# Mixer weights of a Conformer and attention trunk: loaded plainly by SyncE and rounded by ScalarE, where GpSimd's queue rounded them in the transfer

## The chip, the cores and the metric

One core of a Trainium2 chip runs the whole program. The metric is device time in microseconds, the median of several executions. "The profile" is one execution taken by the hardware profiler, with its trace.

## What is computed

Two layers; tokens are 512 plus 16 learned meta tokens, the width D is 1024, D_FF is 2816.

```python
for i in range(DEPTH):
    h_res = h_res + 0.5 * swiglu(rms_norm(h_res, ffn1_norm[i]), ffn1_w_in[i], ffn1_w_out[i])
    h = rms_norm(h_res, mix_norm[i])
    proj = h @ w_in[i]
    y_a = conv_module(proj[..., :o_conv], conv_w[i], conv_b[i], conv_ln_g[i],
                      conv_ln_b[i], conv_w_out[i])
    q = rms_norm(proj[..., o_conv:o_q].reshape(B, L, N_Q_HEADS, HEAD_DIM), q_norm[i])
    k = rms_norm(proj[..., o_q:o_k].reshape(B, L, N_KV_HEADS, HEAD_DIM), k_norm[i])
    v = proj[..., o_k:o_v].reshape(B, L, N_KV_HEADS, HEAD_DIM)
    y_b = window_sink_attention(q, k, v, attn_sinks[i]) @ attn_w_out[i]
    gates = jax.nn.sigmoid(proj[..., o_v:] + gate_bias[i])
    merged = gates[..., :D_MODEL] * y_a + gates[..., D_MODEL:] * y_b
    h_res = h_res + merged @ w_out[i]
    h_res = h_res + 0.5 * swiglu(rms_norm(h_res, ffn2_norm[i]), ffn2_w_in[i], ffn2_w_out[i])
return h_res[:, N_META:]
```

The convolution module is a gated unit, a causal depthwise convolution over 31 tokens, a LayerNorm, a swish and a product. Attention sees a window of two chunks of 64 tokens, the meta tokens and a sink for each head. The part between the two SwiGLUs is called a mixer here.

## The kernel before

**Products.** Every large product is made of three: each operand is split into a part `h` rounded to the matmul's type (fp32r) and the rest `l`, and TensorE adds `wh·xh + wh·xl + wl·xh` in PSUM. So weights have two copies in SBUF, `wha`/`whb` (rounded) and `wla`/`wlb` (rest); `wfa`/`wfb` is the same memory as `wha`/`whb`, seen as plain float32.

**A mixer's blocks.** A mixer is 68 blocks of weights, each 1024x128 (512 KB, in SBUF 128 partitions of 1024 values). Blocks 0 to 43 are the input projection, in four groups of 11; in each group TensorE places the attention of four heads between the blocks. Blocks 44 to 51 are the attention's output, 52 to 59 the convolution's output, 60 to 67 `w_out`. TensorE takes a block in `products` (L1074), 48 matmuls of 264 columns, or 24 of 512 where the second layer drops the meta tokens. PSUM holds the results of two blocks in turn, so block n can start only when VectorE has taken the result of block n - 2: in attention's output at L1848, in `w_out` at L1676.

**Weights.** A block has one of four places in SBUF (`mix_units`). Place n % 4 is free when TensorE is through with block n - 4 (`mix_freed`). Then:

- `mix_hi` (L615), on GpSimd's queue: a transfer that casts float32 to fp32r on its way into `wha`;
- `neg` (L666), on ScalarE: `wla` becomes minus `wha`;
- `mix_lo` (L619), on GpSimd's queue: a transfer of the same block that adds into `wla`, which leaves the rest.

GpSimd issues `mix_hi` of block n ahead of `mix_lo` of block n - 1. A wait for a free place thus also holds back the `mix_lo` behind it.

**ScalarE's order** is written out by hand. `neg` of block n stands among the steps of earlier blocks: in a group through the little function `h(i)`, which is `neg` of the block three after block i, and after the groups through `block_hi(n)`, which is `neg(l, n + 1)`. Between them stand the exponentials (L883), the copies of the turned probabilities (`take_windows` L893, `take_metas` L900 and L902), and in the LayerNorm the squares (L1015), the square root (L1020), the swish (L1025) and the rounding of its result (L1028). After L902 TensorE multiplies the probabilities with the values (`mix_values`, L1310 and L1313), three times in a group: after its ninth block, in the middle of its eleventh, and after the first block of the next group. VectorE's loop in the LayerNorm scales by the reciprocal (L1889), takes the rest of each swish result (L1892), and behind the eighth takes two blocks of attention's output (`take_att`, L1848).

**The SwiGLUs' weights** go another way: SyncE's queue loads `raw` pairs of tiles (L543 768 KB, L546 256 KB) and output weights (L552) as plain float32. ScalarE rounds them (L675, L697, L704) and ScalarE or VectorE makes the rest (L679, L1475). Near the end of a mixer ScalarE and VectorE also prepare the first pairs of the second SwiGLU. In a mixer SyncE otherwise copies the keys to the upper partitions (`kw`, L578), once a group, as soon as VectorE has them.

Of the kernel before, what the change touches and what calls it, by code (L numbers as in the profile page):

```python
# [25 lines left out]
ACT = mybir.ActivationFunctionType  # L26
# [3 lines left out]
P = 128  # L30
DEPTH, D, SEQ, META = 2, 1024, 512, 16
CHUNK, HD, CONV_K = 64, 64, 31
# [4 lines left out]
KD, KF = D // P, FF // P  # L37

CHUNKS = ((0, 11), (11, KF))
# [7 lines left out]
GROUPS = NKV  # L47
# [27 lines left out]
GB_N = 11  # L75
# [9 lines left out]
B_CONV, B_MO = B_ATT + KD, B_ATT + 2 * KD  # L85
NBLK = B_MO + KD
# [66 lines left out]
def run_of(j):  # L153

    s = j // KF
    while not begins(s):
        s -= 1
    e = s + 1
    while e < STAGES and not begins(e):
        e += 1  # L160
    return s * KF, e * KF
# [39 lines left out]
USED = {key: n + 3 for n, key in enumerate(tensor_order())}  # L201
# [28 lines left out]
def mix_freed(l, n):  # L230
    if n > 3:
        return USED["mix", l, n - 4]
    if n == 0:
        return USED["P4", (2 * l + 1) * KF - 1]
    if REGION[(2 * l + 1) * KF - 1] == 0:
        return USED[("P7", "P2", "P6")[n - 1], (2 * l + 1) * KF - 1]
    return USED["out", 2 * l, len(CHUNKS) - 1, NB - 4 + n]
# [16 lines left out]
def build(nc, x, params, qk_gain, sinks, pairs, outs6, outs5, mixes, out):  # L254
# [7 lines left out]
    with ctx:  # L262
        def sb(name, shape, dt=F32, at=ctx):
            return at.enter_context(nc.sbuf_tensor(name, shape, dt))

        def sem(name):
            return ctx.enter_context(nc.semaphore(name))
# [44 lines left out]
        mix = ExitStack()  # L312
# [5 lines left out]
        kw = sb("kw", [P, META + NCH * WK], at=mix)  # L318
# [65 lines left out]
        def units(bufs, u, n):  # L384

            t, u = (bufs[0], u) if u < BASE_UNITS else (bufs[1], u - BASE_UNITS)
            return t[:, u:u + n, :, :].rearrange("p u k c -> p (u k) c")

        hi_units, lo_units, f32_units = (wha, whb), (wla, wlb), (wfa, wfb)
# [45 lines left out]
        def mix_units(bufs, n):  # L435
            return units(bufs, MIX_UNITS[n % 4], 2)
# [13 lines left out]
            return ap.rearrange("p k (h n) -> p (k h) n", h=2)  # L450


        w_hi, w_neg = [sem(f"w_hi{s}") for s in range(4)], sem("w_neg")
        w_lo = [sem(f"w_lo{s}") for s in range(4)]
        raw_in, raw22_in = [sem(f"raw_in{s}") for s in range(2)], [sem(f"raw22_in{s}") for s in range(2)]
        prm_in, first_lo, sq_used = sem("prm_in"), sem("first_lo"), sem("sq_used")
# [10 lines left out]
        blk_used = sem("blk_used")  # L467
# [14 lines left out]
        qrms_ready, krms_ready, kn_ready = sem("qrms_ready"), sem("krms_ready"), sem("kn_ready")  # L482
        kn_dup = sem("kn_dup")
# [45 lines left out]
        @block.sync  # L529
        def _(sp):  # L530

            def load_x(k):
                sp.dma_start(resid[:, k, :], x[:, k, :]).then_inc(x_in[k], 16)

            def load_pair(j):

                j0, j1 = run_of(j)
                if j - 2 >= j0:
                    sp.wait_ge(a_hi, j - 1)
                    sp.wait_ge(s_sum, 4 * (j - 1))  # L540
                if j in (2, 3):
                    sp.wait_ge(first_lo, j)
                sp.dma_start(raw[:, j % 2, KP:4 * KP, :], pairs[j, :, KP:4 * KP, :]).then_inc(raw_in[j % 2], 16)  # L543
                if j - 2 >= j0:
                    sp.wait_ge(a22_hi, j - 1)
                sp.dma_start(raw[:, j % 2, 0:KP, :], pairs[j, :, 0:KP, :]).then_inc(raw22_in[j % 2], 16)  # L546

            def load_out(s, c, m):
                count, u, k = out_block(s, c, m)
                sp.wait_ge(blk_used, out_freed(s, c, m))  # L550
                src = (outs6, outs5)[m % 2][(count - 1) // 2, :, :, :]
                sp.dma_start(units(f32_units, u, 2)[:, 0:k, :], src).then_inc(ob_in[m % 3], 16)  # L552

            def stage(s):
                for c, (ta, tb) in enumerate(CHUNKS):
                    for t in range(ta, tb):
                        j = s * KF + t
                        if j + 2 < run_of(j)[1]:
                            load_pair(j + 2)
                        if t == tb - 2:  # L560
                            load_out(s, c, 0)
                        if t == tb - 1:
                            load_out(s, c, 1)
                            load_out(s, c, 2)
                    for b in range(NB - 3):
                        load_out(s, c, b + 3)

            load_x(0)
            load_x(1)
            load_pair(0)  # L570
            for k in range(2, KD):
                load_x(k)
            load_pair(1)
            for l in range(DEPTH):
                stage(2 * l)
                for g in range(GROUPS):
                    sp.wait_ge(kn_ready, l * GROUPS + g + 1)
                    sp.dma_start(kw[HD:P, :], kw[0:HD, :]).then_inc(kn_dup, 16)  # L578

                sp.wait_ge(blk_used, USED["mix", l, B_CONV])  # L580
                load_pair((2 * l + 1) * KF)
                load_pair((2 * l + 1) * KF + 1)
                stage(2 * l + 1)

            for m in range(KD):
                sp.wait_ge(res_done, (STAGES * len(CHUNKS) - 1) * KD + m + 1)
                sp.dma_start(out[:, m, :], resid[:, m, META:]).then_inc(fin_out, 16)
            sp.wait_ge(fin_out, 16 * KD)


        @block.gpsimd
        def _(pool):
            nc.gpsimd.memset(eps64[:, :], HD * EPS).then_inc(const_done, 1)
            nc.gpsimd.memset(ident[:, :], 0.0).then_inc(const_done, 1)
            nc.gpsimd.memset(ones[:, :], 1.0).then_inc(const_done, 1)
            nc.gpsimd.memset(eps1[:, :], EPS).then_inc(const_done, 1)
            pool.wait_ge(const_done, 4)
            nc.gpsimd.affine_select(out=ident[:, :], in_=ident[:, :], compare_op=ALU.not_equal, fill=1.0,
                                    base=0, pattern=[[-1, P]], channel_multiplier=1).then_inc(const_done, 1)

            def base_lo(j):
                pool.wait_ge(a_neg, j - 1)
                pool.dma_start(units(lo_units, U_A[REGION[j]], 2), pairs[j, :, KP:3 * KP, :], accum_op=ALU.add)\
                    .then_inc(a_lo[j % 2], 16)

            def base22_lo(j):
                pool.wait_ge(a22_neg, j)
                pool.dma_start(units(lo_units, U_A22[REGION[j]], 1), pairs[j, :, 0:KP, :], accum_op=ALU.add)\  # L610
                    .then_inc(a22_lo[j % 2], 16)

            def mix_hi(l, n):
                pool.wait_ge(blk_used, mix_freed(l, n))
                pool.dma_start(mix_units(hi_units, n), mixes[l * NBLK + n, :, :, :]).then_inc(w_hi[n % 4], 16)  # L615

            def mix_lo(l, n):
                pool.wait_ge(w_neg, l * NBLK + n + 1)
                pool.dma_start(mix_units(lo_units, n), mixes[l * NBLK + n, :, :, :], accum_op=ALU.add)\  # L619
                    .then_inc(w_lo[n % 4], 16)  # L620

            def stage(s):
                for c, (ta, tb) in enumerate(CHUNKS):
                    j0, j1 = s * KF + ta, s * KF + tb
                    more = j1 < run_of(j0)[1]
                    for j in range(j0, j1):
                        if j + 2 < j1:
                            base_lo(j + 2)
                        if j + 1 < j1:
                            base22_lo(j + 1)  # L630
                    if more:
                        base_lo(j1)
                        base22_lo(j1)
                        base_lo(j1 + 1)

            for l in range(DEPTH):
                stage(2 * l)
                mix_hi(l, 0)
                mix_lo(l, 0)
                mix_hi(l, 1)  # L640
                for n in range(2, NBLK):
                    mix_hi(l, n)
                    mix_lo(l, n - 1)
                    if n == B_MO + 5:
                        base_lo((2 * l + 1) * KF)
                mix_lo(l, NBLK - 1)
                base22_lo((2 * l + 1) * KF)
                base_lo((2 * l + 1) * KF + 1)
                stage(2 * l + 1)
# [3 lines left out]
        def _(act):  # L653
            func = nc.scalar.activation
# [5 lines left out]
            def neg(l, n):  # L660

                if n >= NBLK:
                    return
                s, turn = mix_turn(l, n)
                act.wait_ge(w_hi[s], turn * 16)
                func(mix_units(lo_units, n), mix_units(hi_units, n).bitcast(F32), ACT.Copy, scale=-1.0)\  # L666
                    .then_inc(w_neg, 1)

# [277 lines left out]
            for l in range(DEPTH):  # L946
# [52 lines left out]
                g = GROUPS - 1  # L999
# [963 lines left out]
```

## Time and profile before

| | |
|---|---|
| median of 3 runs | 2389.26 us (2387.78 to 2391.06) |
| the profiled execution | 2391.75 us |
| its span, first to last instruction | 2390.0 us |
| mean granted TensorE clock | 0.990 of 2.4 GHz |
| busy: TensorE, VectorE, ScalarE, GpSimd | 2347.2, 1680.6, 1223.8, 345.4 us |
| moved by GpSimd's queue, by SyncE's queue | 210.53 MB, 145.08 MB |

The mixers run from about 384 to 856 us and from 1579 to 2037 us, the four SwiGLUs before, between and after them. Busy times count instructions, not waits. In the rows of the profile a line number is that of the kernel before; in a timeline the value in brackets is how long the engine stood idle just ahead of the row, and what ended that.

### The profile page before, as it was taken

The numbers are of one execution on the slowest core, as the hardware profiler recorded it, in microseconds if no ns is written. First come the engines' busy times: TensorE is split into PE (matmuls) and PEld (weight loads), VectorE is DVE, ScalarE is ACT, GpSimd is POOL, SyncE is SP. The second block draws the span as 40 slices with busy tenths as digits, with TensorE's granted clock in tenths as the row PEclk, the third lists the DMA queues.
The fourth block names the chain that finished last, engine by engine and source line by source line (L and its number), as shares of the span: only waits on it lengthen the run. The fifth ranks groups of instructions, "written<-read, shape, count | busy, mean of one in ns | idle before, by whom it ended". The sixth has DMA issues, their size and how long they took to land.

```text
span 2390.0 us, 43268 instructions
## 1 busy us (share of the span) xinstructions
PE 2347.2 (98%) x17809; PEld 2232.3 (93%) x17809; DVE 1680.6 (70%) x2732; ACT 1223.8 (51%) x1987; POOL 345.4 (14%) x454
## 2 busy tenths in 40 slices
PE   7999999999999999999999999999999999999999
PEld 6999999999999999999999999999888777898997
DVE  8855854898886478568678558548988855874773
ACT  7734733443445377356467347343434354762751
POOL 1101101111212211011011011011211222110110
PEclk9999999999999999999999999999999999999999
DMA  6845736666667968458458457366776698683753
GB/s 171 183 122 145 168 88 152 147 147 146 149 141 186 214 129 184 112 144 185 110 122 183 126 143 170 88 151 147 151 158 143 139 219 195 141 197 104 164 130 113
DMA packets 111364, 358.70 MB, mean 150 GB/s; under 512 B 12608, under 2 KB 12608, under 8 KB 111168
## 3 DMA queue, kind: packets, MB, share of 16 engines
q0 software_dynamic: 64080, 210.53, 43.2%
q1 hardware_dynamic: 46720, 145.08, 21.1%
q8 instruction: 141, 2.31, 0.4%
q14 instruction: 55, 0.45, 0.1%
q10 hardware_dynamic: 368, 0.33, 0.0%
HBM read 351.41 MB, written 2.10 MB: 148 GB/s over the span
## 4 chain that ended last, share of the span: by engine, by line
PE 85%; DVE 6%; ACT 4%; DMA 3%; issue 2%; DVEq 0%; ACTq 0%; SPq 0%
PE po L1074 27%; PE po L1091 22%; PE po L1142 20%; PE ptr L1091 7%; PE pov L1091 4%; DMA wha<-in_mixes 1%; DVE cv L1691 1%; DMA wla<-in_mixes 1%; PE pov L1310 1%; PE pov L1313 1%; PE pstat L1270 1%; PE pov L1240 1%; DMA wfa<-in_outs 1%; DVE rms L1540 1%; PE ptr L1279 1%
## 5 line engine op out<-in xcount | busy, mean ns | idle before, releaser
L1074 PE MATMUL po<-xh,wha 128*128 128x264 f32 (+1 forms) x1408 | 351.3, 316 | 2.4 <-DMA wla<-in_mixes 1.7
L1074 PE MATMUL po<-xl,wha 128*128 128x264 f32 (+1 forms) x1408 | 341.4, 309 | 0.0
L1074 PE MATMUL po<-xh,wla 128*128 128x264 f32 (+1 forms) x1408 | 339.7, 308 | 0.0
L1691 DVE SCALAR_TENSOR_TENSOR cv<-ub,lp,cv 128x528 f32<-128x528 f32 (+1 forms) x480 | 333.4, 754 | 1.7
L1142 PE MATMUL po<-hh,wha 128*128 128x264 f32 (+1 forms) x1232 | 282.8, 299 | 1.9 <-DVE wla L1483 1.9
L1142 PE MATMUL po<-hl,wha 128*128 128x264 f32 (+1 forms) x1232 | 283.7, 300 | 0.0
L1142 PE MATMUL po<-hh,wla 128*128 128x264 f32 (+1 forms) x1232 | 283.7, 300 | 0.0
L666 ACT ACTIVATE wla<-wha 128x1024 fp32r<-128x1024 f32 x136 | 143.7, 1058 | 232.2 <-DMA wha<-in_mixes 232.1
L1483 DVE TENSOR_TENSOR wla<-wfa,wha 128x768 fp32r<-128x768 f32 (+1 forms) x128 | 113.6, 890 | 202.9 <-ACT wha L704 202.8
L1074 PEld LDWEIGHTS po<-xh,wha 128*128 128x128 f32 x1408 | 232.1, 193 | 23.1 <-issue 6.1
L1074 PEld LDWEIGHTS po<-xh,wla 128*128 128x128 f32 x1408 | 231.3, 192 | 11.5
L1074 PEld LDWEIGHTS po<-xl,wha 128*128 128x128 f32 x1408 | 231.8, 192 | 10.3
L704 ACT ACTIVATE wha<-wfa 128x768 fp32r<-128x768 f32 (+1 forms) x128 | 101.0, 789 | 267.7 <-DMA wfa<-in_outs 267.7
L1091 PE MATMUL po<-x7h,whb 128*128 128x264 f32 (+1 forms) x768 | 221.0, 288 | 17.1 <-ACT tmp L710 6.9
L1091 PE MATMUL po<-x7h,wha 128*128 128x264 f32 (+1 forms) x832 | 236.4, 284 | 0.5 <-DVE tmp L1571 0.5
L1091 PE MATMUL po<-x7l,wha 128*128 128x264 f32 (+1 forms) x832 | 236.4, 284 | 0.0
L1091 PE MATMUL po<-x7h,wla 128*128 128x264 f32 (+1 forms) x832 | 236.0, 284 | 0.0
L1091 PE MATMUL po<-x7l,whb 128*128 128x264 f32 (+1 forms) x768 | 218.1, 284 | 0.0
L1091 PE MATMUL po<-x7h,wlb 128*128 128x264 f32 (+1 forms) x768 | 217.8, 284 | 0.0
L1142 PEld LDWEIGHTS po<-hh,wha 128*128 128x128 f32 x1232 | 196.1, 188 | 10.5 <-DVE wla L1483 2.6
L1142 PEld LDWEIGHTS po<-hh,wla 128*128 128x128 f32 x1232 | 196.9, 189 | 7.5
L1142 PEld LDWEIGHTS po<-hl,wha 128*128 128x128 f32 x1232 | 196.4, 188 | 7.6
(239 smaller groups left out, 5665.6 us busy)
## 6 DMA issues: line engine op xcount, KB each, us to landing
wha<-in_mixes POOLq DMA_DIRECT2D x136, 512.0 KB, 4.4
wla<-in_mixes POOLq DMA_DIRECT2D x136, 512.0 KB, 6.5
raw<-in_pairs SPq DMA_DIRECT2D x88, 768.0 KB, 5.3
wfa<-in_outs SPq DMA_DIRECT2D x64, 384.0 KB, 3.1
wlb<-in_pairs POOLq DMA_DIRECT2D x47, 512.0 KB, 8.6
raw<-in_pairs SPq DMA_DIRECT2D x88, 256.0 KB, 7.0
wla<-in_pairs POOLq DMA_DIRECT2D x87, 256.0 KB, 6.7
wfa<-in_outs SPq DMA_DIRECT2D x64, 320.0 KB, 2.9
```

The costliest lines, as they stand in the source:

```text
L666: func(mix_units(lo_units, n), mix_units(hi_units, n).bitcast(F32), ACT.Copy, scale=-1.0)\
L704: func(units(hi_units, u, 2)[:, 0:k, :], units(f32_units, u, 2)[:, 0:k, :], ACT.Copy).then_inc(ob_hi, 1)
L1074: ins = mm(po[:, 2 * out_slot + h, 0:width], w[:, k, :], v[:, k, t:t + width], start=begin and k == 0 and p == 0, stop=last and k == kt - ...
L1091: ins = mm(bank, a[:, kp, :], b[:, kp, cols7], start=begin and kp == 0 and p == 0, stop=kp == KP - 1 and p == 2, skip_group_check=True)
L1142: ins = mm(po[:, 2 * ps(m) + h, 0:width], w[:, k, :], v[:, t, x:x + width], start=t == 0 and p == 0, stop=t == CHUNK_T - 1 and p == 2, ski ...
L1240: mm(qss[:, pos, :], qsq[:, tok0(pos):tok0(pos) + CHUNK, :].rearrange("p n j -> p (n j)"), halves[:, :], start=True, stop=True)
L1270: ins = mm(score(i, h), q[r, :], kw[r, c:c + WK], start=True, stop=True)
L1279: ins = tr(ptr[:, (2 * n + h) * P:(2 * n + h + 1) * P], pw[:, (b + 1) % 2, at:at + WIN], ident[:, :])
L1310: mm(dst[h * HD:(h + 1) * HD], vw[:, pos - 1, :], cut(pt[:, i, h, :]), start=True, stop=False, skip_group_check=True)
L1313: ins = mm(dst[h * HD:(h + 1) * HD], vz[0:n, i - i0, h, :], cut(ptm[0:n, :]), start=pos == 0, stop=True, skip_group_check=True)
L1483: tt(units(lo_units, u, 2)[:, 0:k, :], units(f32_units, u, 2)[:, 0:k, :], units(hi_units, u, 2)[:, 0:k, :].bitcast(F32), ALU.subtract).the ...
L1691: stt(cv[:, j, a:], u, w, cv[:, j, a:], ALU.mult, ALU.add).then_inc(conv_step, 1)
```

## The change

SyncE's queue loads each mixer block as plain float32 into its place (`load_mix`, into `wfa`, the memory of `wha`), still after `mix_freed`. ScalarE rounds it in place to fp32r, and then negates it into `wla` as before. GpSimd's queue keeps the accumulating transfer alone, in the order of the blocks. On SyncE's queue the load of block 0 goes between the output weights of the first SwiGLU; the others follow its last, and the key copies and the first two pairs of the second SwiGLU get places between the loads.

```diff
@@ @block.sync
+            def load_mix(l, n):
+
+                sp.wait_ge(blk_used, mix_freed(l, n))
+                sp.dma_start(mix_units(f32_units, n), mixes[l * NBLK + n, :, :, :]).then_inc(w_in[n % 4], 16)
+
@@
                     for b in range(NB - 3):
                         load_out(s, c, b + 3)
+                        if b == 0 and s % 2 == 0 and c == len(CHUNKS) - 1:
+                            load_mix(s // 2, 0)
@@
             for l in range(DEPTH):
                 stage(2 * l)
-                for g in range(GROUPS):
-                    sp.wait_ge(kn_ready, l * GROUPS + g + 1)
-                    sp.dma_start(kw[HD:P, :], kw[0:HD, :]).then_inc(kn_dup, 16)
-
-                sp.wait_ge(blk_used, USED["mix", l, B_CONV])
-                load_pair((2 * l + 1) * KF)
-                load_pair((2 * l + 1) * KF + 1)
+                for n in range(NBLK):
+                    if n:
+                        load_mix(l, n)
+                    g, i = divmod(n, GB_N)
+                    if g < GROUPS and i == 8:
+                        sp.wait_ge(kn_ready, l * GROUPS + g + 1)
+                        sp.dma_start(kw[HD:P, :], kw[0:HD, :]).then_inc(kn_dup, 16)
+
+                    if n in (B_CONV + 4, B_CONV + 6):
+                        load_pair((2 * l + 1) * KF + (n - B_CONV - 4) // 2)
                 stage(2 * l + 1)
@@ @block.gpsimd
-            def mix_hi(l, n):
-                pool.wait_ge(blk_used, mix_freed(l, n))
-                pool.dma_start(mix_units(hi_units, n), mixes[l * NBLK + n, :, :, :]).then_inc(w_hi[n % 4], 16)
@@
-                mix_hi(l, 0)
-                mix_lo(l, 0)
-                mix_hi(l, 1)
-                for n in range(2, NBLK):
-                    mix_hi(l, n)
-                    mix_lo(l, n - 1)
-                    if n == B_MO + 5:
+                for n in range(NBLK):
+                    mix_lo(l, n)
+                    if n == B_MO + 4:
                         base_lo((2 * l + 1) * KF)
-                mix_lo(l, NBLK - 1)
@@ @block.scalar, in neg(l, n)
-                act.wait_ge(w_hi[s], turn * 16)
+                act.wait_ge(w_in[s], turn * 16)
+                func(mix_units(hi_units, n), mix_units(f32_units, n), ACT.Copy).then_inc(w_hi, 1)
+                act.wait_ge(w_hi, l * NBLK + n + 1)
                 func(mix_units(lo_units, n), mix_units(hi_units, n).bitcast(F32), ACT.Copy, scale=-1.0)\
                     .then_inc(w_neg, 1)
```

ScalarE's order from the first mixer's LayerNorm on, before: the end of the squares (L1015), the square root into `t`, and the first steps of swish (`cv`) and rounding (`xh`).

```order
L1015 ACTIVATE pw<-cv 128x528 x3
L666 ACTIVATE wla<-wha 128x1024
L1020 ACT_TABLE_LOAD
L1020 ACTIVATE t<-pstat,eps 128x528
L666 ACTIVATE wla<-wha 128x1024
L1025 ACT_TABLE_LOAD
...
L1028 ACTIVATE xh<-cv 128x528
L666 ACTIVATE wla<-wha 128x1024
L1025 ACTIVATE cv<-cv,lp 128x528
```

And of the change, the same place (its lines are three higher, L666 is L669):

```order
L1018 ACTIVATE pw<-cv 128x528 x3
L667 ACTIVATE wha<-wfa 128x1024
L669 ACTIVATE wla<-wha 128x1024
L1023 ACT_TABLE_LOAD
L1023 ACTIVATE t<-pstat,eps 128x528
L667 ACTIVATE wha<-wfa 128x1024
L669 ACTIVATE wla<-wha 128x1024
L1028 ACT_TABLE_LOAD
...
L1031 ACTIVATE xh<-cv 128x528
L667 ACTIVATE wha<-wfa 128x1024
L669 ACTIVATE wla<-wha 128x1024
L1028 ACTIVATE cv<-cv,lp 128x528
```

Each negation has a copy just ahead of it, and nothing else has moved on ScalarE.

SyncE's queue through the first mixer, before: the last output weights of the first SwiGLU, the keys, and the pairs (L543 and L546) of the second SwiGLU.

```order
L552 DMA wfa<-in_outs 128x640
L578 DMA kw<-kw 64x1168 x4
L543 DMA raw<-in_pairs 128x1536
L546 DMA raw<-in_pairs 128x512
L543 DMA raw<-in_pairs 128x1536
L546 DMA raw<-in_pairs 128x512
L543 DMA raw<-in_pairs 128x1536
```

And of the change:

```order
L552 DMA wfa<-in_outs 128x640
L557 DMA wfa<-in_mixes 128x1024 x8
L589 DMA kw<-kw 64x1168
...
L589 DMA kw<-kw 64x1168
L557 DMA wfa<-in_mixes 128x1024 x15
L543 DMA raw<-in_pairs 128x1536
L546 DMA raw<-in_pairs 128x512
L557 DMA wfa<-in_mixes 128x1024 x2
L543 DMA raw<-in_pairs 128x1536
L546 DMA raw<-in_pairs 128x512
L557 DMA wfa<-in_mixes 128x1024 x9
L543 DMA raw<-in_pairs 128x1536
```

A key copy now stands behind the load of its group's ninth block, the first two pairs are two blocks apart, and the third pair stands behind the mixer's last load.

## Rows read from the trace of the kernel before

**Rows 1.** The page: busy time of each engine, its share of the span, instructions

```profile
PE 2347.2 (98%) x17809; PEld 2232.3 (93%) x17809; DVE 1680.6 (70%) x2732; ACT 1223.8 (51%) x1987; POOL 345.4 (14%) x454
```

**Rows 2.** TensorE's waits: engine, output, line <- releaser: us in total, times, longest

```profile
PE po L1074 <- DVE resid L1676: 2.0, 2, 1.4
...
PE po L1074 <- DMA wla<-in_mixes: 1.7, 4, 0.6
...
PE po L1074 <- DVE gb L1848: 0.6, 1, 0.6
```

**Rows 3.** The page's groups: count, busy us, mean ns, idle before and its releaser

```profile
L666 ACT ACTIVATE wla<-wha 128x1024 fp32r<-128x1024 f32 x136 | 143.7, 1058 | 232.2 <-DMA wha<-in_mixes 232.1
```

**Rows 4.** ScalarE's timeline, rounding and negation of a pair: start us, us, instruction

```profile
820.28 1.05 ACT L675 ACTIVATE whb<-raw 128x1024 fp32r<-128x1024 f32 x1
821.36 1.06 ACT L679 ACTIVATE wlb<-whb 128x1024 fp32r<-128x1024 f32 x1
```

**Rows 5.** The page's DMA issues: queue, count, KB each, median us to landing

```profile
wha<-in_mixes POOLq DMA_DIRECT2D x136, 512.0 KB, 4.4
...
raw<-in_pairs SPq DMA_DIRECT2D x88, 768.0 KB, 5.3
wfa<-in_outs SPq DMA_DIRECT2D x64, 384.0 KB, 3.1
```

**Rows 6.** Timelines of ScalarE, VectorE and TensorE through the first mixer's LayerNorm

```profile
740.43 0.70 ACT L1020 ACTIVATE t<-pstat,eps 128x528 f32<-128x528 f32 x1 [0.87 <-PE pstat L1369]
...
746.01 0.83 ACT L1025 ACTIVATE cv<-cv,lp 128x528 f32<-128x528 f32 x1 [1.89 <-DVE cv L1889]
...
750.33 1.05 ACT L666 ACTIVATE wla<-wha 128x1024 fp32r<-128x1024 f32 x1
...
759.45 0.71 DVE L1892 TENSOR_TENSOR xl<-cv,xh 128x528 fp32r<-128x528 f32 x1 [1.64 <-ACT xh L1028]
760.08 0.70 DVE L1848 SCALAR_TENSOR_TENSOR gb<-gb,po 128x528 f32<-128x528 f32 x1
...
760.83 0.51 PE L1074 MATMUL po<-xh,wha 128*128 128x264 f32 x2
```

**Rows 7.** Timelines of ScalarE and TensorE in the first mixer's attention

```profile
529.12 0.25 ACT L902 ACTIVATE ptm<-ptr 96x128 f32<-96x128 f32 x1
...
529.98 0.31 PE L1313 MATMUL pov<-ptm,vz 96*64 96x32 f32 x4
...
551.56 1.06 ACT L666 ACTIVATE wla<-wha 128x1024 fp32r<-128x1024 f32 x1 [3.05 <-DMA wha<-in_mixes]
...
552.79 0.26 ACT L902 ACTIVATE ptm<-ptr 96x128 f32<-96x128 f32 x1
...
553.14 0.45 PE L1310 MATMUL pov<-pt,vw 128*64 128x128 f32 x4
...
693.10 0.31 PE L1313 MATMUL pov<-ptm,vz 96*64 96x32 f32 x4 [1.24 <-ACT ptm L902]
```

**Rows 8.** Timelines of ScalarE and TensorE at the first mixer's start

```profile
390.38 2.00 ACT L666 ACTIVATE wla<-wha 128x1024 fp32r<-128x1024 f32 x2
...
397.31 0.48 PE L1074 MATMUL po<-xh,wha 128*128 128x264 f32 x2 [0.26 <-DMA wla<-in_mixes]
```

**Rows 9.** Timelines of SyncE's and GpSimd's queues and TensorE, first group's keys

```profile
420.34 0.53 SPq L578 DMA_DIRECT2D kw<-kw  x1
...
422.50 0.56 POOL L615 DMA_DIRECT2D wha<-in_mixes  x1 [11.42 <-PE po L1074]
...
428.00 0.40 PE L1272 MATMUL pstat<-kw,qb 64*128 64x16 f32 x4
```

**Rows 10.** Timelines of ScalarE and TensorE near the end of the first mixer

```profile
834.17 1.06 ACT L666 ACTIVATE wla<-wha 128x1024 fp32r<-128x1024 f32 x1 [3.63 <-DMA wha<-in_mixes]
...
838.10 0.51 PE L1074 MATMUL po<-mh,wha 128*128 128x264 f32 x2 [0.61 <-DVE resid L1676]
```

**Rows 11.** One stretch by windows: busy us and count by engine, granted clock, DMA share, GB/s

```profile
470.00:550.00 80.00, 80.00 (x681) 77.33 (x681) 71.06 (x121) 34.37 (x81) 15.78 (x22) 0.96 0.67 143
```

More of the change, by code:

```diff
@@ L450, in two1 @@
             return ap.rearrange("p k (h n) -> p (k h) n", h=2)
-        w_hi, w_neg = [sem(f"w_hi{s}") for s in range(4)], sem("w_neg")
+        w_in, w_hi, w_neg = [sem(f"w_in{s}") for s in range(4)], sem("w_hi"), sem("w_neg")
         w_lo = [sem(f"w_lo{s}") for s in range(4)]
```

## The prediction

> **What bounds the kernel now.** I read the page first. TensorE is busy for 98% of the span [rows 1], so a change can save only what TensorE waits for, and costs whatever makes it wait more. Second, TensorE's own waits [rows 2]. All the waits that the mixers' weights could cause are small: 1.7 us for landings of `wla` in four places, 2.0 us for VectorE to free a PSUM slot (L1676) in two, 0.6 us for the same at L1848 in one. Third, ScalarE. The negation at L666 takes 1.06 us a block, 136 times, and ScalarE idled 232 us ahead of it for landings of `wha` [rows 3]. That idle time looks like cover for another copy. But an average doesn't say where the idle time lies; in some places the steps behind L666 on ScalarE are those TensorE comes to with no slack. So, fourth, I read the timeline at the few places where a mixer is tight.
>
> **The edit, part by part.** All queues do the same for each of the 68 blocks of a mixer. POOL loses one issue, SP gains one, ScalarE gains one copy.
>
> *The copy.* The nearest row is another pair of rounding and negation of 128x1024, L675 and L679: started 1.08 us apart, each 1.04 to 1.06 us long [rows 4]. So a block costs ScalarE 1.08 us more: 136 x 1.08 = 147 us. ScalarE is busy for only half of the span [rows 1], so its total doesn't bound; only order does.
>
> *The load.* On POOL, 512 KB land 4.4 us after issue. On SP's queue, 384 KB land in 3.1 and 768 KB in 5.3 us [rows 5]. Between them 512 KB come to 3.1 + 2.2/3 = 3.8 us: 0.6 us sooner. The bounds are those two rows. So where ScalarE waited for the landing, its negation ends 1.08 - 0.6 = 0.5 us later (bounds -0.2 and +2.0); where it did not wait, 1.08 us later. The accumulating transfer is then issued at once, where POOL now often stands at the next block's wait first; for most blocks that gives the 0.5 us back, and it costs nothing.
> The Trainium skill speaks against that 0.6 us: "DMA: Bandwidth & Descriptors", section "Rules for kernel authors", says that spreading transfers over the issuing engines saves only issue time, since all run on the same 16 DMA engines. By the rule the load would come some 0.2 us sooner, and the sum below would be near 14 us instead of 11. I stay with the rows, since they are landings of this kernel.
>
> *The LayerNorm of the convolution branch, +6.0 us.* This is the largest term. ScalarE's order there holds six of the negations. At the square root (L1020) ScalarE had 0.87 us idle [rows 6]. Ahead of it come a copy for a block whose load it waits for (+0.5, which the squares carry on as about +0.6) and one for which it doesn't wait (+1.08): 0.6 + 1.08 - 0.87 = 0.8 us late. The copy right behind the root hides in the 1.89 us that ScalarE idles before L1025. In the eight steps of L1025 and L1028 ScalarE is the slower engine: VectorE waits 1.64 us for the last `xh`. Two negations stand between those steps, at 750.33 and once more four steps later; their copies add 2 x 1.08 = 2.2. VectorE then frees PSUM at L1848 from 760.08 to 760.78, and TensorE starts the convolution's output blocks at 760.83 [rows 6]: no slack. In one mixer TensorE already waits 0.6 us there [rows 2]. So 0.8 + 2.2 = 3.0 us a mixer reach TensorE: 6.0. Bounds: 2 x 2.2 if the root is not late; 2 x 3.9 if no idle time helps.
>
> *Attention, +5.7 us.* The probabilities' last copy (L902) stands right behind a negation, and TensorE needs it at once. At a group's end, ScalarE waits 3.05 us for a landing, negates, copies until 553.05; TensorE starts on it at 553.14 [rows 7]. Six such places have gaps of 0.1 to 0.7 us, three of them 0.1 or 0.2; +0.5 gives 0.4 + 0.4 + 0.3 and three zeros: 1.1. After a group's ninth block, L902 ends at 529.37 and TensorE starts at 529.98 [rows 7]; six such gaps are 0.2 to 0.6 us, and there ScalarE hardly waits for a landing: +0.8 against them gives 2.4. In each mixer's fourth group TensorE already waits for it, 1.24 us at 693.10 [rows 7]: +1.08 twice, 2.2. Together 5.7; bounds 2.2 (only the fourth groups) and 15 (1.08 us at fourteen places).
>
> *A mixer's first blocks, +2.2 us.* Behind the first square root the negations of blocks 2 and 3 run together, 2.00 us from 390.38; their loads landed long before. Block 2 then waits 0.26 us for its transfer [rows 8]. Its accumulation starts 1.08 us later, in two mixers. Bounds 1 and 4, as block 3's may be late too.
>
> *Keys copied across, +0.4 us.* SP copied `kw` at 420.34. Now the ninth load stands ahead of it, and waits for block 4, which ended just before 422.50; the scores start at 428.00 [rows 9]. So the copy is issued some 2.4 us later and behind 512 KB. Bounds 0 (the later groups have over 3 us) and 2.
>
> *Pair weights of the second SwiGLU, -3.0 us.* At 834.17 ScalarE had idled 3.63 us for a `wha` that shared the engines with the third pair; a rounding, VectorE and the slot at L1676 stand behind, and TensorE idles 0.61 us at 838.10 [rows 10]. The second mixer's 1.4 is the rest of the 2.0 [rows 2]. SP now sends that pair only after its last mixer load, so I take both as gone: -2.0. The first two pairs went out together, and now stand two blocks apart; of the 1.7 us of waits for `wla` I give back 1.0. Bounds 0 and -3.7.
>
> Sum: 6.0 + 5.7 + 2.2 + 0.4 - 3.0 = +11.3 us on the profiled execution's 2391.75. The median of the runs, 2389.26, is 2.5 us lower: 2400.6. A measurement of this kernel can tell about 0.2%, 4.8 us, from no change.
>
> **The rivals.**
> *The copies hide.* The load lands 1.1 us sooner or more, so attention's delay shrinks to the fourth groups (2.2), LayerNorm's to 2.2 a mixer, and the first blocks' to 1.0: 2.2 + 4.4 + 1.0 - 3.7 = +3.9, 2393. For it: 232 us of idle time. Against: at 750.33 and before L902 ScalarE wasn't waiting, and no sooner landing helps there.
> *Faster.* Same premise, but LayerNorm isn't what holds TensorE: VectorE reaches L1848 as early as now. All waits for transfers and slots go (-3.7), and one stretch per kernel at the slower clock with them: in the first mixer's second attention group the granted clock was 0.96 over 80 us [rows 11], so 6.4 us at 1.2 GHz, worth 3.2. That gives 2382. It decides if the load lands in 3.3 us or less and ScalarE's steps L1025 and L1028 turn out to be limited by VectorE; their 1.64 us wait speaks against it.
> *Slower still.* New gaps pull the clock down. TensorE standing 3 us at two places and some hundred ns at a dozen could bring two to three more stretches at 1.2 GHz, at 3.2 us each [rows 11]. That is +20, 2409. The Trainium skill has this in "TensorE: Matmul & The Clock Gate", Part 1: the clock is halved when the array was not busy enough. No row here says how much idle is enough.
> *The change doesn't do what it says:* the built order has the copy and SP's loads in place, so I give it nothing.
>
> **How the numbers follow.** Forecast, 2396 to 2406: 0.50. Copies hide: 0.17. Faster: 0.08. Slower still: 0.25. The forecast's likeliest time is 2400.6. Leaving out the faster case and the end of the slow one, the range is 2391 to 2411. Faster by over 0.2%: 0.08, within: 0.17, slower: 0.75.
>
> **What would show it.** A wait of about 3 us of TensorE for L1848's slot in each mixer, and VectorE waiting 2 us longer in all for `xh`. Waits for L902 at ten or more places, none over 2.5 us. The load landing in 3.8 us. No wait near the third block of w_out. No more than 1 us elsewhere. I am wrong if TensorE enters the convolution's output on time, if L902's waits stay at two per mixer, or if PEclk of the mixers moves by more than 0.01.

## The result, and the profile after

| | before | the change |
|---|---|---|
| median of the runs | 2390.16 us (4 runs, 2387.78 to 2392.39) | 2443.95 us (4 runs, 2435.67 to 2446.59) |
| the profiled execution | 2391.75 us | 2435.67 us |
| its span | 2390.0 us | 2433.9 us |
| mean granted TensorE clock | 0.990 | 0.987 |

The change is slower: 1.0217 times before, 95% interval 1.0197 to 1.0237, some 54 us. I had forecast 2400.6 us and a range up to 2411. The direction was right, the size was off by a factor of almost five. The profiled execution of the change is 8 us below its median, so its trace accounts for 43.9 us of the 54. Single runs of 9528.52 us (e4), 4583.1 us (e11) and 3230.2 us (before, beside e9 to e11) are on record, and nothing is read from them.

The page of the change, which answers to [rows 1, 3, 5]. First the busy times, then the chain that ended last, the group of the new copy, and the DMA issues.

```profile
PE 2356.1 (97%) x17809; PEld 2239.3 (92%) x17809; DVE 1681.1 (69%) x2732; ACT 1366.3 (56%) x2123; POOL 269.2 (11%) x318
...
PE 80%; DVE 7%; ACT 6%; DMA 5%; issue 2%; SPq 0%; DVEq 0%; ACTq 0%
...
L667 ACT ACTIVATE wha<-wfa 128x1024 fp32r<-128x1024 f32 x136 | 143.7, 1056 | 168.1 <-DMA wfa<-in_mixes 167.9
...
wfa<-in_mixes SPq DMA_DIRECT2D x136, 512.0 KB, 4.0
```

ScalarE has 142.5 us more work and still idles 168 us for the loads. By its total, 56% of the span where it was 51%, it is still far from being the bound, and a load takes 4.0 us where the cast took 4.4. None of these figures shows a loss of 44 us; the chain only says that TensorE's share of it fell from 85 to 80%. The waits show where. TensorE's waits in the change, in the columns of [rows 2]; left out are rows that stand in both kernels at about the same size:

```profile
PE pov L1313 <- ACT ptm L905: 15.4, 9, 2.4
...
PE pov L1316 <- ACT ptm L905: 7.2, 4, 2.0
PE po L1077 <- DVE gb L1851: 6.7, 2, 3.8
PE pstat L1273 <- DMA kw<-kw: 6.2, 3, 3.7
...
PE pstat L1275 <- DMA kw<-kw: 5.0, 4, 1.8
...
PE po L1077 <- DMA wla<-in_mixes: 3.1, 2, 1.6
```

The copied probabilities (`ptm`) cost 22.6 us where they cost 3.0. The keys (`kw`) cost 11.2 us where they cost nothing. The PSUM place that VectorE frees at L1848 (now L1851), called L1848's place here, costs 6.7 where it was 0.6 [rows 2]. The wait for the one it frees at L1676, 2.0 us before, is gone. All rows of that view together: 38.5 us before, 73.7 us now, +35.2. The rest is mostly the clock: the granted clock was at 1.2 instead of 2.4 GHz for 46.3 us of the span before and for 61.4 us now (that is what the means 0.990 and 0.987 come from; a recorded text below that says 63 counts up to 2 us behind the span's end). By my estimate 15.1 us more at half speed cost 7.5 us, and TensorE's busy time for the same 17809 matmuls did grow by 8.9 us. 35.2 + 7.5 = 42.7 of the 43.9 us. This estimate, **waits plus half the time at 1.2 GHz**, is used for every run below.

### The profile page after: what moved, and what is told of

Its sections match the earlier page's. It is cut to its first block, busy times and chain, and to the rows that moved or that the text cites. A ratio compares the mean times of both kernels' runs of the same rounds, so it can differ in the third digit from the quotient of the medians.

```text
span 2433.9 us, 43404 instructions
## 1 busy us (share of the span) xinstructions
PE 2356.1 (97%) x17809; PEld 2239.3 (92%) x17809; DVE 1681.1 (69%) x2732; ACT 1366.3 (56%) x2123; POOL 269.2 (11%) x318
## 3 DMA queue, kind: packets, MB, share of 16 engines
q0 software_dynamic: 44496, 139.22, 32.9%
## 4 chain that ended last, share of the span: by engine, by line
PE 80%; DVE 7%; ACT 6%; DMA 5%; issue 2%; SPq 0%; DVEq 0%; ACTq 0%
PE po L1077 23%; PE po L1094 22%; PE po L1145 19%; PE ptr L1094 7%; PE pov L1094 5%; DMA wfa<-in_mixes 3%; DVE cv L1694 2%; DMA kw<-kw 2%; ACT wha L667 1%; ACT wla L669 1%; PE pov L1313 1%; PE pstat L1273 1%; PE pov L1316 1%; PE pov L1243 1%; ACT cv L1028 1%
## 5 line engine op out<-in xcount | busy, mean ns | idle before, releaser
L667 ACT ACTIVATE wha<-wfa 128x1024 fp32r<-128x1024 f32 x136 | 143.7, 1056 | 168.1 <-DMA wfa<-in_mixes 167.9
L625 POOL DMA_DIRECT2D wla<-in_mixes x136 | 118.2, 869 | 981.5 <-ACT wla L669 981.5
```

What stands on the lines that cost most here:

```text
L667: func(mix_units(hi_units, n), mix_units(f32_units, n), ACT.Copy).then_inc(w_hi, 1)
```

## The places in the trace

**The keys.** Timeline of the change, SyncE's queue in the first group (start, duration of the issue, queue, line):

```profile
421.13 0.33 SPq L557 DMA_DIRECT2D wfa<-in_mixes  x1
421.50 0.53 SPq L589 DMA_DIRECT2D kw<-kw  x1
```

TensorE's timeline at the same place, the start of the scores:

```profile
428.30 0.40 PE L1275 MATMUL pstat<-kw,qb 64*128 64x16 f32 x4 [1.33 <-DMA kw<-kw]
```

The key copy goes out 0.4 us behind a 512 KB load and lands at 428.26, 6.8 us later; the scores start 0.04 us after that. The same holds in all eight groups. The row of this transfer among the DMA issues of the kernel before (its size, and the median time to landing):

```profile
kw<-kw SPq DMA_DIRECT2D x8, 292.0 KB, 3.1
```

And of the change:

```profile
kw<-kw SPq DMA_DIRECT2D x8, 292.0 KB, 6.9
```

Before, the scores started 2.6 to 5.1 us after the landing. The copy lands 3.8 us later by the median, is issued later too, and all that slack is gone.

The load ahead isn't alone. In five of the eight groups GpSimd had also sent an accumulating transfer 1.1 to 3.3 us ahead of the copy, and it was still in flight. There the copy took 6.8 to 9.1 us, and TensorE waited 10.7 of the 11.2 us. In the other three groups, with only the load ahead, it took 5.1 to 5.7 us, and TensorE waited 0.5 us in all.

**The probabilities.** Timeline of the change, ScalarE near the end of the first group:

```profile
448.05 1.06 ACT L667 ACTIVATE wha<-wfa 128x1024 fp32r<-128x1024 f32 x1 [1.16 <-DMA wfa<-in_mixes]
449.14 1.06 ACT L669 ACTIVATE wla<-wha 128x1024 fp32r<-128x1024 f32 x1
450.11 0.26 ACT L905 ACTIVATE ptm<-ptr 96x128 f32<-96x128 f32 x1
```

TensorE's timeline there:

```profile
450.41 0.31 PE L1316 MATMUL pov<-ptm,vz 96*64 96x32 f32 x4 [1.69 <-ACT ptm L905]
```

Two things happen here. The copy puts L905 1.08 us later, which I had counted. But ScalarE also waits 1.16 us for the load of block 11, where before it did not wait. What is in flight beside that load is shown by the queues. GpSimd's timeline of the kernel before, in the same stretch:

```profile
442.31 0.55 POOL L615 DMA_DIRECT2D wha<-in_mixes  x1 [5.46 <-PE po L1074]
442.84 0.91 POOL L619 DMA_DIRECT2D wla<-in_mixes  x1
```

GpSimd's timeline of the change:

```profile
441.43 0.86 POOL L625 DMA_DIRECT2D wla<-in_mixes  x1 [3.71 <-ACT wla L669]
```

And SyncE's queue of the change:

```profile
442.35 6.73 SPq L557 DMA_DIRECT2D wfa<-in_mixes  x2
```

Before, GpSimd waited for the free place, sent the cast of block 11 at 442.31 and the accumulation of block 10 behind it; the cast landed at 446.58, 4.3 us on. Now GpSimd sends the accumulation of block 10 as soon as its negation is done, at 441.43. That is 0.9 us ahead of the load of block 11, which then lands at 448.03, 5.7 us after its issue. The row of SyncE's queue joins two loads; the first is issued at 442.35.

**The LayerNorm.** Timeline of the change, VectorE at the end of the first mixer's:

```profile
777.69 0.71 DVE L1895 TENSOR_TENSOR xl<-cv,xh 128x528 fp32r<-128x528 f32 x1 [2.72 <-ACT xh L1031]
778.31 1.31 DVE L1851 SCALAR_TENSOR_TENSOR gb<-gb,po 128x528 f32<-128x528 f32 x2
```

And TensorE:

```profile
779.06 0.81 PE L1077 MATMUL po<-xh,wha 128*128 128x264 f32 x2 [2.90 <-DVE gb L1851]
```

VectorE waits 2.72 us for the last `xh`, where it was 1.64 [rows 6], and 2.2 us more over all eight steps, as two copies of 1.08 us would have it. TensorE waits 2.9 us for the place that VectorE frees.

## The experiments

Every loss seen so far has its own place, but they needn't add up. Three theories: **A**, separate waits, each with its own cause, each given back when its cause is mended. **B**, an overload: ScalarE and the queues have less slack everywhere, and a wait mended in one place comes back in another. **C**, the granted clock carries the loss. Times below are medians, ratios are against the kernel before on the same chip, waits and clock are of the profiled run, which lies up to 8 us off its kernel's median, so gains by medians and by profiles differ. The table at the end has all of them.

**e1, the keys ahead of the load.**

```diff
                 for n in range(NBLK):
-                    if n:
-                        load_mix(l, n)
                     g, i = divmod(n, GB_N)
                     if g < GROUPS and i == 8:
                         sp.wait_ge(kn_ready, l * GROUPS + g + 1)
                         sp.dma_start(kw[HD:P, :], kw[0:HD, :]).then_inc(kn_dup, 16)
+                    if n:
+                        load_mix(l, n)
```

> The change with one edit: on SyncE's queue each group's key copy stands ahead of the load of the group's ninth block, not behind it. Theory A (three separate waits, each of its own place): in the changed kernel TensorE waits 11.2 us in seven places for kw; the copy lands in some 3 us again, these waits fall below 1 us, and the time is 10 to 13 us shorter than the changed kernel's 2444, so 2431 to 2434. Theory B (ScalarE or the transfers are simply overloaded in a group, and the wait shows wherever TensorE comes first): the wait for kw turns up again at the copy of the probabilities (L905), and less than 4 us are gained.

2429.88 us, ratio 1.0169 (1.0151 to 1.0187). The key copy again lands in 3.1 us by the median, and its wait falls from 11.2 to 0.4 us. So with the load ahead of it gone the wait is gone; the accumulation ahead alone (the first group of each mixer) still makes the copy take 5.8 and 6.1 us. The median falls by 14 us, a little more than A's 10 to 13, but the profiled span by only 5.0: the waits for the probabilities rise by 3.2 us, those for `wla` by 3.3, and the time at 1.2 GHz from 61.4 to 62.7 us.

**e2, the probabilities ahead of two negations.** `h(0)` and `h(8)` are negations of a later block, with their copies; `take_metas` holds L905. The same is done in the second place, with `h(0)` and `take_metas(l, g - 1, 2)`.

```diff
-                    h(8)
                     take_metas(l, g, 0)
+                    h(8)
```

> The change with one edit: in two places of each group ScalarE copies the turned probabilities (take_metas) ahead of rounding and negating a block, not behind. Theory A: TensorE's waits for that copy, 22.6 us in thirteen places, fall below 4 us; the time is 18 to 22 us shorter than 2444, 2422 to 2426, and the wait for kw stays at about 11. Theory B: less than 8 us are gained, since the next step of ScalarE or the rounded block itself is late instead (waits for wla over 8 us). Theory C (the granted clock carries most of the loss): the time moves with the stretches at 1.2 GHz and not with the waits.

2405.71 us, ratio 1.0071 (1.0048 to 1.0094), 38 us less than the change by the medians and 25 by the profiled runs. All 22.6 us of waits for the probabilities are gone, the keys' rise to 14.2, and the time at 1.2 GHz falls to 53.1 us. By the medians that is far more than A's 18 to 22. This is one order on one engine, and the largest part of the loss.

**e3, both edits.**

> Both edits together, keys first and probabilities first. Theory A: the two add, 29 to 35 us shorter than the changed kernel, 2409 to 2415. Theory B: no more than the larger of the two alone. Theory C: 2430 or more unless the stretches at 1.2 GHz fall from 63 us to 48 or less.

2396.7 us, ratio 1.003 (1.0016 to 1.0045). Both waits are at 0.6 us or less. 47 us of the loss are given back, against 14 and 38 by the edits apart, so these two nearly add. It is more than A's 29 to 35: the time at 1.2 GHz is down to 37.5 us, so by the estimate 12 us of the gain are the clock, which A had left out.

**e4, both, and attention's output taken just ahead of the last step of the LayerNorm.**

```diff
-                take_att(6)
+                    if k == 7:
+                        take_att(6)
```

> Both edits, and VectorE takes attention's seventh output block (L1851) ahead of its last step of the LayerNorm and not behind it. Theory A: TensorE's wait of 6.7 us for that slot goes; 5 to 7 us below e3_both, 2403 to 2409. If the LayerNorm itself is the limit (the rest xl of its last steps), less than 2 us are gained and the wait stands at the next block's slot or at xl.

2391.77 us, ratio 1.0014 (1.0001 to 1.0028). The wait for L1851's place falls from 6.3 to 0.2 us, and the median by 4.9, but the intervals of e3 and e4 overlap and the profiled span doesn't fall (10.3 us more at 1.2 GHz). With three orders mended the change stands 0.14% above the kernel before. Two of the three moves help that kernel too, so this is not yet the change's cost (see e10). Now the two halves of the change, one at a time.

**e5, ScalarE's work alone:** the kernel before, with the negation done twice.

```diff
+                func(mix_units(lo_units, n), mix_units(hi_units, n).bitcast(F32), ACT.Copy, scale=-1.0).then_inc(w_one, 1)
+                act.wait_ge(w_one, l * NBLK + n + 1)
                 func(mix_units(lo_units, n), mix_units(hi_units, n).bitcast(F32), ACT.Copy, scale=-1.0)\
```

> The kernel before with a second negation of each block ahead of the first (into the same tiles, so the result is the same): ScalarE's added work of 1.08 us a block alone, with the weights still loaded and rounded by GpSimd's queue. Theory A (the change's loss is ScalarE's copy plus waits of its own for each moved transfer): the LayerNorm's +6 and the late first blocks' +2 stay, TensorE's waits for the copied probabilities come to 10 to 13 us instead of 22.6, because the loads at the ninth and eleventh blocks still land 4.4 us after their place is free; no wait for the keys; +16 to +24 us, 2406 to 2414. Theory B (the copy is the whole loss, the queue only passes it on): +35 or more, 2425 and up.

2425.71 us, ratio 1.0141 (1.0122 to 1.016): +36, more than A gave, and as much as B said. The probabilities cost 15.5 us, where A said 10 to 13, and L1848's place 7.0, as it said. What A made too small are three other waits: `wla` 6.3 us, L1676's place 4.8, the keys 2.1, 13.2 in all against 3.7 before, where A had only the 2 us of the first blocks.

**e6, the queues alone:** the change without its copy.

```diff
-                func(mix_units(hi_units, n), mix_units(f32_units, n), ACT.Copy).then_inc(w_hi, 1)
-                act.wait_ge(w_hi, l * NBLK + n + 1)
```

> The change without its copy on ScalarE (the rounding of the mixers' weights is left out): the loads on SyncE's queue alone. Theory A: TensorE waits about 11 us for the keys as in the change, 0 to 4 us for the probabilities, 0.6 at L1848's place, the pairs' 2 us stay saved: +8 to +13 us, 2398 to 2403. Theory B: the queue costs nothing as long as ScalarE has its old slack: the keys alone, or less, 2390 to 2396.

2417.62 us, ratio 1.0109 (1.009 to 1.0128): +28, where A said 8 to 13 and B less. So the copy isn't the whole loss, as B had it for e5. The keys alone cost 18.2 us; in all eight groups an accumulation had gone out 0.6 to 4.4 us ahead of their copy. The row of their copy among e6's DMA issues:

```profile
kw<-kw SPq DMA_DIRECT2D x8, 292.0 KB, 7.9
```

The halves make 28.7 and 21.6 us of waits over before, 50.3 together; the whole change makes 35.2. So the two don't add. A likely reason, not tested: a TensorE that already stood for the probabilities comes later to the scores, and waits less for the keys.

**e7, the accumulation held behind the next load.** GpSimd waits for the place of block n + 1 ahead of the accumulation of block n, as the place of `mix_hi` in its queue made it do before the change.

```diff
             def mix_lo(l, n):
+                if n < NBLK - 1:
+                    pool.wait_ge(blk_used, mix_freed(l, n + 1))
                 pool.wait_ge(w_neg, l * NBLK + n + 1)
```

> The change, with GpSimd holding back the accumulating transfer of block n until the place of block n+1 is free, which puts it behind that block's load again, as it was before the change. If the loads at the ninth and eleventh blocks land late because an accumulating transfer is now under way ahead of them (A1): they land 4.5 us or less after their place is free instead of 5 to 6, the probabilities' waits fall from 22.6 to 10 to 14 us, and the time falls by 8 to 14 us, to 2430 to 2436. If something else delays them, the landings stay at 5 to 6 us and the time stays within 4 us of the change's 2444, or rises because the accumulating transfers come later.

2412.87 us, ratio 1.0095 (1.0073 to 1.0116), 31 us less than the change by the medians and 20 by the profiled runs, for one wait added. I had expected 8 to 14. The same place as above in e7's timeline, first GpSimd:

```profile
442.25 0.86 POOL L627 DMA_DIRECT2D wla<-in_mixes  x1 [4.72 <-PE po L1079]
```

SyncE's queue of e7:

```profile
441.92 6.72 SPq L557 DMA_DIRECT2D wfa<-in_mixes  x2
```

And ScalarE of e7:

```profile
446.34 1.07 ACT L669 ACTIVATE wha<-wfa 128x1024 fp32r<-128x1024 f32 x1
```

The load goes first, lands at 445.76, 3.8 us after its issue, and ScalarE no longer waits for it. I took the load ahead of L905 at ten such places (blocks 11, 14, 22, 25, 33, 36 of the first mixer; 11, 14, 25, 36 of the second):

| | accumulations sent ahead of the load and still in flight | load, issue to landing |
|---|---|---|
| before | at four none, else one for its last 0.3 to 1.4 us | 3.7 to 4.4 us |
| the change | at nine one for 2.9 to 5.3 us, at the tenth none | 4.9 to 6.1 us (3.7 at the tenth) |
| e7 | at six none, else one for its last 0.3 to 2.3 us | 3.6 to 5.0 us |

At two more such places, blocks 22 and 33 of the second mixer, the change had one accumulation in flight for 2.6 and 2.7 us, and the load took 3.8 and 3.9 us: no delay shows there.

The waits for the probabilities fall from 22.6 to 12.0 us, those for the keys from 11.2 to 5.6, and the time at 1.2 GHz from 61.4 to 41.2 us. By the estimate, half of the 20 us are the clock. L1676's place costs 2.8 us again.

**e8 and e10, the kernel before with these moves and nothing of the change.** e10 has the edits of e2 and e4's `take_att`; e8 also sends the first pairs of the second SwiGLU apart and holds the third back.

> The kernel before with three moves and nothing of the change: the copied probabilities ahead of the two negations they stood behind, attention's output taken only at the LayerNorm's last step, and the first pairs of the second SwiGLU sent apart. TensorE's waits for the probabilities (3.0 us), for L1848's place (0.6), for L1676's (2.0) and some of those for wla (1.7) go: -5 to -7 us, 2382 to 2385. If ScalarE's later negations make new waits, 2388 to 2392. If clock stretches go too, 2378.

> The kernel before with two of the three moves of the mended one (the copied probabilities ahead of the negations, attention's output at the last step), the pairs left together. TensorE's waits of 3.0 and 0.6 us go, those of 2.0 us at L1676's place and 1.7 for wla stay: -3 to -4 us, 2385.5 to 2387; the spaced pairs are then worth 2 to 3 us of the 6.

e8: 2383.79 us, ratio 0.9964 (0.9949 to 0.9979). e10: 2382.55 us, ratio 0.9968 (0.9955 to 0.9981). Both are faster than before, by 6 to 8 us. For e10 I had expected 3 to 4. Its waits are only 0.6 us below those of before, so by the estimate its gain is the clock (12.2 us less at 1.2 GHz). The two can't be told from each other by their times, and intervals this wide can neither show nor refute the 2 to 3 us I had put on the pairs. The waits do differ: L1676's place costs 2.6 us in e10 and nothing in e8.

e10 is also the kernel to hold the mended change against, since both have the same two moves. e4 is 9 us above it (ratios 1.0014 and 0.9968). So mending the orders doesn't make the change free. What these 9 us are isn't shown.

**e9, the change with all four edits.**

> The change with all four places mended: the keys ahead of the load, the copied probabilities ahead of the two negations, attention's output at the LayerNorm's last step, and GpSimd's accumulating transfer held behind the next block's load. Without the last of these the time was 2391.8. If the order of the two transfers mattered only for the probabilities, the hold gains nothing once these are ahead: 2389 to 2394, waits for wla 5 to 8 us. If it also helps the blocks themselves: wla's waits under 4 us and 2384 to 2388, still not under the mended kernel before (2383.8).

2392.33 us, ratio 1.0008 (0.9998 to 1.0019). e4 without the hold had 2391.77: once nothing urgent stands behind a load on ScalarE, the order of the transfers makes no difference that shows. Measured beside e10 on the same chip, it is 9.8 us slower, and the intervals lie apart.

**e11, ScalarE's work alone (e5) with the two moves of e10.**

> The kernel before with the second negation (ScalarE's added work alone, which cost +36 us) and the same two moves. If that work costs time only through the probabilities and L1848's place (15.5 and 7.0 us of TensorE's waits there), these two waits go and what stays is wla, L1676's place and the keys, 8 to 13 us of waits: 2394 to 2402. If the added work wears down every slack and the waits return elsewhere: 2408 or more.

2399.18 us, ratio 1.0033 (1.002 to 1.0046): 27 us below e5. But the two moves give 8 us to the kernel before by themselves; against e10 the added work costs 17 us, where it cost 36 without the moves. The largest mixer waits left are `wla` 9.3 us and L1676's place 4.9.

The waits of TensorE in each profiled run, in us:

| | median | `ptm` | `kw` | L1848's place | `wla` | L1676's place | all waits | at 1.2 GHz | span |
|---|---|---|---|---|---|---|---|---|---|
| before | 2390.2 | 3.0 | 0 | 0.6 | 1.7 | 2.0 | 38.5 | 46.3 | 2390.0 |
| the change | 2444.0 | 22.6 | 11.2 | 6.7 | 3.1 | 0 | 73.7 | 61.4 | 2433.9 |
| e1 keys first | 2429.9 | 25.8 | 0.4 | 6.3 | 6.4 | 0 | 68.0 | 62.7 | 2428.9 |
| e2 probabilities first | 2405.7 | 0 | 14.2 | 6.5 | 3.3 | 0.2 | 52.3 | 53.1 | 2409.0 |
| e3 both | 2396.7 | 0.6 | 0.4 | 6.3 | 3.7 | 0.3 | 42.0 | 37.5 | 2390.0 |
| e4 and the place | 2391.8 | 0 | 0.4 | 0.2 | 7.2 | 0.2 | 37.2 | 47.8 | 2390.7 |
| e5 copy alone | 2425.7 | 15.5 | 2.1 | 7.0 | 6.3 | 4.8 | 67.2 | 45.0 | 2419.7 |
| e6 queues alone | 2417.6 | 5.9 | 18.2 | 0.6 | 4.2 | 0 | 60.1 | 51.2 | 2415.8 |
| e7 load ahead | 2412.9 | 12.0 | 5.6 | 6.1 | 4.5 | 2.8 | 61.4 | 41.2 | 2414.1 |
| e8 before, three moves | 2383.8 | 0.7 | 0 | 0 | 0.4 | 0 | 32.9 | 41.0 | 2381.3 |
| e9 change, all four | 2392.3 | 2.1 | 0 | 0 | 8.8 | 0.6 | 39.9 | 27.3 | 2384.6 |
| e10 before, two moves | 2382.6 | 1.3 | 1.5 | 0 | 2.7 | 2.6 | 37.9 | 34.1 | 2384.8 |
| e11 copy, two moves | 2399.2 | 0.9 | 0.4 | 0.7 | 9.3 | 4.9 | 46.8 | 41.0 | 2398.5 |

Against before, waits plus half the time at 1.2 GHz meet the span's difference within 1.8 us in nine of the twelve runs and within 3.8 in the other three (e7, e9, e11). So A and B are each half right: the places and causes are separate and each answers to its own edit (A), but what an edit gives back is less or more than its wait, since a TensorE that comes sooner to one place meets the next wait (B, e1 and the halves). C is the smaller part in the change, 7.5 of 43.9 us, but half of e7's gain and by the profile all of e10's.

## Why the prediction was right and wrong

**LayerNorm, +6.0: right.** The wait at L1848's place went from 0.6 to 6.7 us, +6.1, for the reason given; e4 removes it by taking that result sooner, ahead of the last step.

**Pair weights, -3.0: -3.1.** L1676's waits, 2.0 us, are gone, and so are two of the four for `wla`: 0.46 us at 1962.24 and 0.62 at 1968.65 before, in the second mixer's convolution output. That the pairs' new places did it fits e8 and e10, but e7 has those places too and 2.8 us for L1676's place.

**A mixer's first blocks, +2.2: right, +2.4.** The other two waits for `wla` stand at the named third block of each mixer. They were 0.26 and 0.41 us, and are 1.53 (at 397.62) and 1.56 us (at 1612.29). One reading was off: block 3's load landed at 390.67, not long before its negation.

**Attention, +5.7: wrong, +19.6 us.** It lies above the bound of 15. The step that failed is in the part on the load: that the accumulating transfer issued at once "costs nothing", and that the load comes 0.6 us sooner wherever ScalarE waits for it. The mean held: over blocks 4 to 43 of both mixers the load landed 0.5 us sooner after its place was free (4.82 us before, 4.30 after). It failed just at the blocks that matter. There the accumulation of the block before goes out ahead of the load, and the load takes 4.9 to 6.1 us. e7 puts the order back and the term becomes +9.0: 3.3 us over my 5.7, within its bounds. At the fourth groups, where I had put +2.2, the change's waits are 3.0 us and were 2.9, so nearly all of the 19.6 lies at the eleven other places; there e7 leaves 5.0 us, near my 3.5, and the fourth groups take 7.0. The copy's own price was too low as well where the load comes no sooner: e5, with the queues of before, has +12.5.

I set the Trainium skill's rule ("DMA: Bandwidth & Descriptors", section "Rules for kernel authors": spreading transfers over issuing engines saves only issue time) against the rows, and chose the rows. The means don't decide between them. From issue to landing the load took 4.49 us before and 4.27 after, 0.2 us less, as by the rule; the other 0.3 lies ahead of the issue. With the order restored (e7) it took 4.01, 0.5 us less, near the rows. The rule's reason, that all transfers share the same 16 DMA engines and interleave, agrees with the table of e7, and I ought to have carried it on to the question of which transfer is in flight beside which.

**Keys, +0.4: wrong, +11.2 us.** I put the issue 2.4 us later and wrote that the later groups "have over 3 us". I counted the later issue and left out the 512 KB ahead of the copy, though I named it: the copy's landing went from 3.1 to 6.9 us, against 2.6 to 5.1 us of slack. e1 shows it by putting the copy first. The step that failed in attention is at work here too: where no accumulation had gone out ahead, the waits were 0.5 of the 11.2 us, and e7, with the load still ahead of the copy, halves them to 5.6.

**Elsewhere, "No more than 1 us":** held in the change. It would not have held for the copy alone (e5).

**The clock.** I gave 0.25 to new gaps bringing two to three stretches more at 1.2 GHz. There are 15.1 us more of them, 7.5 us of time by the estimate, about what that rival said; the mixers' granted clock moved by less than 0.01. As the one reason for a slower result it was the wrong rival: the waits themselves were five times as large. The change did what it says, and the copies did not hide.

**The sum.** The terms that I had made 6.0 + 5.7 + 2.2 + 0.4 - 3.0 = 11.3 measure 6.1 + 19.6 + 2.4 + 11.2 - 3.1 = 36.2, and the clock, which the sum put at nothing, 7.5. The last 10 us of the 54 aren't in the profiled run. The change's other three runs have mean clocks of 0.985, 0.985 and 0.986, 7 to 12 us more at 1.2 GHz than the profiled one; that would be some 3 to 6 us of the 6 to 11 by which they are longer. It is a rough estimate, and a mean clock alone doesn't give a time: one run of the kernel before had 0.941 and took 2395.14 us. The rest stays open.

## What to carry to other kernels

When a transfer moves to another queue, write down for every urgent landing which transfers are now issued just ahead of it, on either queue: the old shared queue may have kept an order that nobody wrote down, and here one wait on GpSimd that restored it brought back 31 of 54 us. Before work is added to an engine that idles, move what another engine waits for ahead of it; two such moves took the cost of ScalarE's added work from 36 to 17 us, and made the kernel before itself 8 us faster. That gain belongs to the moves, not to the change: a mended change has to be held against a kernel before that has the same moves, and here it is still 9 us slower. A sum of separate terms needs bounds wide enough for waits that grow where there was slack: with the copy alone, three small ones grew by 9.5 us.

## What the runs showed of the hardware

- A 292 KB copy from SBUF to SBUF with nothing sent just ahead of it landed in 3.0 to 3.4 us (seven of eight before, the eighth 5.1; six in e1). With an accumulation sent 1.4 us ahead it took 5.8 and 6.1 (e1), 0.4 us behind a 512 KB load on the same queue 5.1 to 5.7, and behind both 6.8 to 9.1 (the change).
- A 512 KB plain load landed in 3.6 to 5.0 us with no accumulation sent ahead of it, or only the end of one, and in 4.9 to 6.1 us with one in flight for 2.9 us or more that the other queue had sent ahead; with one in flight for 2.6 and 2.7 us it was 3.8 and 3.9. These are the twelve places named at e7.
- An accumulation sent 0.3 us behind the load at 441.92 (e7) left the load at 3.8 us; sent 0.9 us ahead of it (the change) it made 5.7.
